# A four-layer model on one core: padding behind the vectors, later rotary angles, and latents that keep their root to the end

## The reference

```
def mla_mixer(hn, positions, w_down, q_norm, kv_norm, w_uq, w_ukv, w_o):
    c = hn @ w_down                                   # 1024 -> 384 + 256 + 32
    cq, ckv, kr = jnp.split(c, [MLA_Q_RANK, MLA_Q_RANK + MLA_KV_RANK], axis=-1)
    q  = rmsnorm_2(cq, q_norm)   @ w_uq               # 16 heads of 64 + 32
    kv = rmsnorm_2(ckv, kv_norm) @ w_ukv              # 16 heads of 64 (keys) + 64 (values)
    q_nope, q_rope = jnp.split(q, [MLA_NOPE], axis=-1)
    k_nope, v      = jnp.split(kv, [MLA_NOPE], axis=-1)
    q = concat(q_nope, apply_rope(q_rope, positions))
    k = concat(k_nope, apply_rope(kr, positions) for every head)
    o = causal_softmax_attention(q, k, v, 1 / sqrt(96))
    return o @ w_o
def rmsnorm_2(x, g):
    return x * rsqrt(mean(x * x) + 1e-6) * g
```

## Time and profile before

| | |
|---|---|
| median of 3 runs | 1326.67 us (1326.57 to 1328.77) |
| profiled execution | 1328.3 us, its span 1326.5 us |
| PE busy | 1301.6 us, 98% |
| DVE busy | 914.5 us, 69% |
| ACT busy | 756.9 us, 57% |
| DMA engines, mean | 220.61 MB in all, 166 GB/s |
| granted TensorE clock, mean | 0.994 |

### The profile page before, as it was taken

The page is one execution under the profiler, slowest core; times in us unless marked ns, Lnnn a source line. Parts: engine busy times, 40 slices in busy tenths (PEclk is TensorE's granted clock), DMA queues, the critical chain, the costliest instruction groups (busy, mean ns, idle before and its releaser), DMA issues.

```text
span 1326.5 us, 29295 instructions
## 1 busy us (share of the span) xinstructions
PE 1301.6 (98%) x12212; PEld 1269.2 (96%) x12212; DVE 914.5 (69%) x1296; ACT 756.9 (57%) x981; POOL 44.1 (3%) x37
## 2 busy tenths in 40 slices
PE   9999999999999999999999999999999999999997
PEld 8999999998999999999989899999999889999997
DVE  4779776488479876468746377666488879666556
ACT  6657665367657665357554266554376776554444
POOL 1010000010010000010000010000001001000000
PEclk9999999999999999999999999999999999999999
DMA  8455554545345555535401136553634335555520
GB/s 332 176 206 191 190 190 190 190 191 193 126 159 191 190 190 190 190 122 191 160 34 45 57 135 223 190 187 133 230 131 183 124 127 207 191 190 190 190 96 32
DMA packets 31980, 220.61 MB, mean 166 GB/s; under 512 B 3712, under 2 KB 3840, under 8 KB 6160
## 3 DMA queue, kind: packets, MB, share of 16 engines
q1 hardware_dynamic: 30672, 213.36, 44.3%
q0 software_dynamic: 784, 4.85, 1.1%
q10 hardware_dynamic: 432, 1.05, 0.2%
HBM read 218.20 MB, written 1.05 MB: 165 GB/s over the span
## 4 chain that ended last, share of the span: by engine, by line
PE 85%; DVE 9%; ACT 4%; issue 1%; DMA 1%; POOL 0%; SPq 0%; DVEq 0%; ACTq 0%; POOLq 0%
PE ps L1845 21%; PE ps L1846 21%; PE ps L1847 21%; PE ps L1856 17%; DVE w_lo L1104 3%; PE ps L1851 2%; PE ps L1852 1%; PE ps L1853 1%; ACT w_hi L504 1%; DVE xt L1156 1%; PE ps L2067 1%; DMA raw<-stream 1%; DVE xA L1166 1%; DVE xB L1166 0%; DVE xB L1128 0%
## 5 line engine op out<-in xcount | busy, mean ns | idle before, releaser
L1104 DVE TENSOR_TENSOR w_lo<-raw,w_hi 128x2048 fp32r<-128x2048 f32 x197 | 449.5, 2287 | 147.1 <-ACT w_hi L504 146.7
L504 ACT ACTIVATE w_hi<-raw 128x2048 fp32r<-128x2048 f32 x197 | 375.9, 1913 | 171.1 <-PE ps L1847 165.1
L1845 PE MATMUL ps<-xB,w_hi 128*128 128x256 f32 x1120 | 314.3, 281 | 1.7 <-DVE up_acc L1230 1.7
L1846 PE MATMUL ps<-xB,w_hi 128*128 128x256 f32 x1120 | 312.8, 279 | 0.0
L1847 PE MATMUL ps<-xB,w_lo 128*128 128x256 f32 x1120 | 312.7, 279 | 0.0
L1845 PEld LDWEIGHTS ps<-xB,w_hi 128*128 128x128 f32 x1120 | 210.5, 188 | 3.2 <-DVE up_acc L1230 1.9
L1845 PE MATMUL ps<-xA,w_hi 128*128 128x256 f32 x744 | 211.0, 284 | 1.6 <-ACT ml_v L1020 1.1
L1846 PEld LDWEIGHTS ps<-xB,w_hi 128*128 128x128 f32 x1120 | 210.5, 188 | 0.1
L1847 PEld LDWEIGHTS ps<-xB,w_lo 128*128 128x128 f32 x1120 | 210.5, 188 | 0.0
L1846 PE MATMUL ps<-xA,w_hi 128*128 128x256 f32 x744 | 207.7, 279 | 0.0
L1847 PE MATMUL ps<-xA,w_lo 128*128 128x256 f32 x744 | 207.6, 279 | 0.0
(11 more groups left out here) (287 smaller groups left out, 1869.3 us busy)
## 6 DMA issues: line engine op xcount, KB each, us to landing
raw<-stream SPq DMA_DIRECT2D x199, 1024.0 KB, 4.8
raw<-stream SPq DMA_DIRECT2D x4, 512.0 KB, 7.8
at_bias<-rel POOLq DMA_DIRECT2D x1, 2048.0 KB, 8.3
hT<-x_t SPq DMA_DIRECT2D x4, 256.0 KB, 7.0
lora_w<-lora POOLq DMA_DIRECT2D x1, 1024.0 KB, 5.1
out_t<-xt SPq DMA_DIRECT2D x4, 256.0 KB, 2.4
hcon<-hyc POOLq DMA_DIRECT2D x1, 576.0 KB, 4.1
wsT<-wst ACTq DMA_DIRECT2D x1, 512.0 KB, 4.3
```

Source lines behind the costliest of these rows:

```text
L504: nc.scalar.activation(w_hi[c.slot][:], raw[c.slot][:], ACT.Copy).then_inc(hi_made, 1)
L1104: nc.vector.tensor_tensor(w_lo[c.slot][:], raw[c.slot][:], w_hi[c.slot][:].bitcast(F32), ALU.subtract).then_inc(lo_made, 1)
L1845: nc.tensor.matmul(out, wh, xh, start=start, stop=False, skip_group_check=True)
L1846: nc.tensor.matmul(out, wh, xl, start=False, stop=False, skip_group_check=True)
```

## The change

`vec` gets 62 unused columns. It then is 3072 bytes, and all tiles behind it begin on a multiple of 1024 bytes from the first tile. `rope_angles` and the sine move behind the loop that splits the first eight chunks. The tile `ml_c` becomes `ml_tok` of the same size, of which six columns are used. The query latents are multiplied by their gain alone, straight from PSUM (ACT the high part, DVE the rest, `rest_query`), and queries are made from them without the root. `token_sums` gets the query root, and the finished key root, with one number a token on the partitions, by products with one column. The value products use the unscaled key latents, and `v_copy` multiplies by the key root. `query_root` refines the query root and leaves it negated in `ml_tok`; it goes into the maximum (one more operation of `biased_max`) and as scale into the exponent. `K_BANK` and `V_BANK` change, since banks 0 and 2 now hold the latents for longer, and PE's waits with them.

```
@@ -87 +87 @@
 GATE_BANK = (4, 6, 7, 5)
-K_BANK, V_BANK, O_BANK = (0, 1, 2, 3, 7, 0, 1, 2), (3, 7, 0, 1), (0, 1, 6, 7)
+K_BANK, V_BANK, O_BANK = (3, 7, 0, 1, 2, 3, 7, 0), (1, 2, 3, 7), (0, 1, 6, 7)
 UNITS = ((0, 1), (1, 2), (2, 4), (4, 6), (6, 8))
@@ -138 +138 @@
         hT = sb("hT", [P, KD, T])
-        vec = sb("vec", [P, NV])
+        vec = sb("vec", [P, NV + 62])
         eye_ones = sb("eye_ones", [P, 2 * P])
@@ -184 +184 @@
-                ml_c = sb("ml_c", [P, 5, T], where=f)
+                ml_tok = sb("ml_tok", [P, 5 * T], where=f)
...
@@ -608 +607 @@
                 d0 = C0[f"dn{f}"]
+                with act.Fori(0, 2) as it:
+                    for s in range(RING):
+                        split_hi(Chunk(d0 + s, it).ahead())
                 if f == 2:
...
                     nc.scalar.activation(ml_cs[:], ml_ang, ACT.Sin).then_inc(cs_made, 1)
-                with act.Fori(0, 2) as it:
-                    for s in range(RING):
-                        split_hi(Chunk(d0 + s, it).ahead())
                 if f >= 2:
@@ -627 +626 @@
                         n = 4 * m + 2 * i + t
-                        last = nc.scalar.activation(pr[:, i, lo:hi], pr[:, i, lo:hi], ACT.Exp, scale=-1.0,
-                                                    bias=st[:, 0, n:n + 1], accum_out=st[:, 1, n:n + 1])
+                        last = nc.scalar.activation(pr[:, i, lo:hi], pr[:, i, lo:hi], ACT.Exp,
+                                                    scale=ml_tok[:, t:t + 1] if a else -1.0, bias=st[:, 0, n:n + 1], accum_out=st[:, 1, n:n + 1])
                 last.then_inc(exp_made, 1)
@@ -1000 +999 @@
                 two = ps[:, s, 0:n * T].rearrange("p (b t) -> p b t", b=n)
-                nc.scalar.activation(ml_c[:, b:b + n, :], two, ACT.Copy)
                 nc.scalar.activation(xt[:, b:b + n, :], two, ACT.Square).then_inc(c_evac, 1)
+                for k, h in ((((2, 0),), (), ((0, 0), (1, 1)))[s]):
+                    nc.scalar.activation(xA[:, k, 0, :], half(s, h), ACT.Copy, scale=col("q_norm", k)).then_inc(lq_hi, 1)
                 if s < 2:
...
-            def latent_root(j, nth):
-                act.wait_ge(c_ss, nth)
-                inverse_root(ml_rs[j], half(4 + j, 0), (384, 256)[j], c_rs)
-            def round_latent(k, nth):
-                act.wait_ge(c_made, nth)
-                nc.scalar.activation(xA[:, k if k < 3 else k + 2, 0, :], xt[:, k, :], ACT.Copy).then_inc(c_hi, 1)
+            def latent_roots():
+                act.wait_ge(c_ss, 2)
+                own.mark(nc.scalar.activation(ml_tok[:, 0:2], ps[:, 4, 0:2], ACT.Ln, bias=col("eps"), scale=1.0 / 384))
+                own.mark(nc.scalar.activation(ml_tok[:, 2:4], ps[:, 4, 2:4], ACT.Copy))
+                own.wait()
+                nc.scalar.activation(ml_tok[:, 0:2], ml_tok[:, 0:2], ACT.Exp, scale=-0.5).then_inc(c_rs, 1)
...
                 t, n = divmod(i, 2)
-                nc.scalar.activation(ml_v[:, t, 512 * n:512 * n + 512], ps[:, V_BANK[i], :], ACT.Copy).then_inc(ml_evac, 1)
+                nc.scalar.activation(ml_v[:, t, 512 * n:512 * n + 512], ps[:, V_BANK[i], :], ACT.Copy,
+                                     scale=ml_tok[:, 2 + t:3 + t]).then_inc(ml_evac, 1)
@@ -1030 +1031 @@
             split_nope_hi(Chunk(c0 + 1).ahead())
-            latent_root(1, 1)
+            act.wait_ge(c_ss, 1)
+            inverse_root(ml_rs[1], half(5, 0), 256, c_rs)
             split_hi(Chunk(c0 + 2).ahead())
             latent(2)
-            round_latent(3, 1)
-            round_latent(4, 2)
-            latent_root(0, 2)
             split_hi(Chunk(c0 + 3).ahead())
+            latent_roots()
             act.wait_ge(fold_done, 1)
...
             v_copy(1)
-            for k in range(3):
-                round_latent(k, 3 + k)
             split_hi(Chunk(c0 + 4).ahead())
@@ -1260 +1258 @@
                 d0 = C0[f"dn{f}"]
-                if f == 2:
-                    rope_angles()
                 with dve.Fori(0, 2) as it:
...
                         split_lo(Chunk(d0 + s, it).ahead())
+                if f == 2:
+                    rope_angles()
                 if f >= 2:
@@ -1288 +1286 @@
-            def biased_max(a, m, bias, sign):
+            def biased_max(a, m, bias, sign, by=None):
@@ -1299 +1297 @@
                                                               ALU.add, ALU.min, st[:, 0, n:n + 1])
+                if by is not None:
+                    link(last)
+                    mx = st[:, 0, 4 * m:4 * m + 4].rearrange("p (i t) -> p i t", t=2)
+                    last = nc.vector.scalar_tensor_tensor(out=mx, in0=mx, scalar=-1.0,
+                                                          in1=by.unsqueeze(1).broadcast_to([P, 2, 2]), op0=ALU.mult,
+                                                          op1=ALU.mult)
                 last.then_inc(max_made, 1)
@@ -1732 +1736 @@
-            def scale_latent(j, nth):
-                dve.wait_ge(c_rs, nth)
-                refine(ml_rs[j], half(4 + j, 0), (384, 256)[j], ml_pr[1][:, 0, 0:T])
-                for k in ((0, 1, 2), (3, 4))[j]:
-                    gain = col("q_norm", k) if j == 0 else col("c_norm", k - 3)
-                    nc.vector.scalar_tensor_tensor(out=xt[:, k, :], in0=ml_c[:, k, :], scalar=gain, in1=ml_rs[j],
-                                                   op0=ALU.mult, op1=ALU.mult).then_inc(c_made, 1)
-            def rest_latent(k, nth):
-                dve.wait_ge(c_hi, nth)
-                x = xA[:, k if k < 3 else k + 2]
-                nc.vector.tensor_tensor(x[:, 1, :], xt[:, k, :], x[:, 0, :].bitcast(F32), ALU.subtract).then_inc(c_lo, 1)
+            def rest_query(nth, k, s, h):
+                dve.wait_ge(lq_hi, nth)
+                nc.vector.scalar_tensor_tensor(out=xA[:, k, 1, :], in0=half(s, h), scalar=col("q_norm", k),
+                                               in1=xA[:, k, 0, :].bitcast(F32), op0=ALU.mult,
+                                               op1=ALU.subtract).then_inc(lq_lo, 1)
+            def query_root():
+                dve.wait_ge(c_rs, 2)
+                y, tmp = ml_tok[:, 0:2], ml_tok[:, 4:6]
+                link(nc.vector.tensor_tensor(tmp, y, y, ALU.mult))
+                link(nc.vector.scalar_tensor_tensor(out=tmp, in0=ps[:, 4, 0:2], scalar=EPS * 384, in1=tmp, op0=ALU.add,
+                                                    op1=ALU.mult))
+                link(nc.vector.tensor_scalar(tmp, tmp, 0.5 / 384, -1.5, ALU.mult, ALU.add))
+                link(nc.vector.tensor_tensor(y, y, tmp, ALU.mult))
@@ -1760 +1767 @@
             def ml_max(m):
-                biased_max(1, m, lambda i, t: ml_bias[:, P:T] if t == 0 else ml_bias[:, 0:T], 1.0)
+                biased_max(1, m, lambda i, t: ml_bias[:, P:T] if t == 0 else ml_bias[:, 0:T], 1.0, ml_tok[:, 0:2])
@@ -1772 +1779 @@
             nc.vector.tensor_tensor(ml_kr[64:128, :], half(1, 1)[64:128], ml_cs[64:128, :], ALU.mult).then_inc(kr_made, 1)
+            rest_query(1, 2, 0, 0)
             split_nope_lo(Chunk(c0 + 1).ahead())
             scale_early(N_ML, 2, c0 + 2, 2)
-            scale_latent(1, 1)
-            k_scale(0)
-            k_scale(1)
-            rest_latent(3, 1)
-            rest_latent(4, 2)
-            k_scale(2)
-            k_scale(3)
+            dve.wait_ge(c_rs, 1)
+            refine(ml_rs[1], half(5, 0), 256, ml_pr[1][:, 0, 0:T])
+            rest_query(3, 0, 2, 0)
+            rest_query(3, 1, 2, 1)
+            for m in range(4):
+                k_scale(m)
             split_lo(Chunk(c0 + 2).ahead())
...
                 k_scale(m)
-            scale_latent(0, 2)
             split_lo(Chunk(c0 + 3).ahead())
-            for k in range(3):
-                rest_latent(k, 3 + k)
+            query_root()
             split_lo(Chunk(c0 + 4).ahead())
@@ -2383 +2388 @@
-            def latent_sums(j, evacs):
-                ks = ((0, 1, 2), (3, 4))[j]
-                pe.wait_ge(c_evac, evacs)
-                for k in ks:
-                    last = plain(half(4 + j, 0), ones, xt[:, k, :], k == ks[0], k == ks[-1])
+            def latent_sums():
+                pe.wait_ge(c_evac, 2)
+                plain(half(5, 0), ones, xt[:, 3, :], True, False)
+                plain(half(5, 0), ones, xt[:, 4, :], False, True).then_inc(c_ss, 1)
+            def token_sums():
+                pe.wait_ge(k_evac, 1)
+                for t in range(2):
+                    plain(ps[:, 4, 2 + t:3 + t], ml_rs[1][:, P * t:P * t + P], eye[:, 0:1], t == 0, True)
+                for t in range(2):
+                    for k in range(3):
+                        last = plain(ps[:, 4, t:t + 1], xt[:, k, P * t:P * t + P], ones[:, 0:1], False, k == 2)
                 last.then_inc(c_ss, 1)
...
             early_pair(N_ML, Chunk(c0), Chunk(c0 + 1), 5)
-            wide_chunk(Chunk(c0 + 2), 2, early_tile(N_ML), None, {5: lambda: latent_sums(1, 2)})
```

(21 more changed lines are left out.)

3 lines of the change are left out of this document (removed).

## The result

The changed kernel takes 1349.35 us (median of 4 runs, 1348.05 to 1350.38) against 1327.16 of the kernel before (4 runs, 1326.57 to 1328.77): a ratio of 1.0165, 95% interval 1.0152 to 1.0178. It is slower by 22 us, where 4.5 us faster was forecast. The time lies outside the range that the prediction gave. The profiled execution took 1349.58 us with a span of 1347.8.

The account below looks back on a forecast made before the run. PE, busy 98%, was taken as the bound, through matmul start-to-start time and holes. Terms -2.10 (angles), -1.56 (latents), -0.80 (padding) sum to -4.46 us: 1326.67 becomes 1322.2, range 1318.0 to 1326.0.

Parts of the forecast that it names:

- Part 1, the padding: Aligning tiles behind the vectors: nothing for products with stationary weights, -0.8 us from 480 256-column products with moving weights.
- the 512 form: Products with 512 moving weight columns, aligned: 233.04 ns, 116.52 per 256, read as no gain or loss from moving-operand alignment.
- Rival B: Big products: both operands starting on one multiple of 1024 slows 7704 matmuls to 118.36 ns; +12.9 us, 1335.9; chance 0.06.
- Part 2: Third block's down projection: moving the angles behind the weight splits removes PE's whole hole near 920 us, -2.10 us.
- Part 3: Latent stage, from first key product to first query product: making latents without the root saves 1.56 us.
- the fold: Fold product after the key products no longer waits for the third latent's square: 0.43 us stays, 0.98 goes.
- the sums: Token sums in the latent stage: 16 one-column instructions take 1.79 us instead of 1.30, so +0.49.
- the -1.37: First query product no longer waits for `v_copy(2)`, its bank being free some 5 us earlier: -1.37 us.
- the new wait of 0.3: Fifth key product waits for both `rest_query(3)` on DVE: +0.3 us.
- C: Latent stage gives nothing back, through dear one-column sums or a late split for the value product: 1324.6 us; chance 0.14.
- E: Attention: each of eight maxima comes 1.8 us later, PE stands 1.0 us eight times: 1330 us; chance 0.03.
- A: Big products: the aligned moving operand gains too, 7704 matmuls each 1.67 ns shorter; -12.9 us, 1309.3; chance 0.08.

Follow-up runs that it names:

- e1: The kernel before with only the 62 unused columns behind the vectors added: 1351.88 us, ratio 1.0184.
- m1: No full kernel: 45 groups of 24 or 48 matmuls, other engines idle, operand starts varied; 256 columns took 120.0 ns at distance 0, 113.4 at 64.
- e6: The kernel before with the later angles alone, no unused columns and the old latents: 1325.83 us, ratio 0.998.
- e7: The kernel before with the rootless latents alone, no unused columns and the old place of the angles: 1326.48 us, ratio 0.9984.
- e5: The changed kernel with 94 unused columns instead of 62, so x starts 128 bytes past a multiple of 1024: 1341.38 us, ratio 1.01 to the kernel before.
- e9: The changed kernel with 110 unused columns instead of 62, so x starts 192 bytes past a multiple of 1024: 1307.29 us, ratio 0.9861 to the kernel before.

## Why the prediction was wrong

- **What bounds the kernel** was right: PE's start-to-start time and its holes. It also named what would prove it wrong, wide steps off by more than 0.2 ns. They are off by 3.3.
- **Part 1, the padding, is the step that failed**: "So I give the wide form nothing." It was carried over from the 512 form (116.52 per 256 columns against 116.69). The two forms do not answer to the place alike: from the old place to the aligned one the 256-column step goes up by 3.3 ns and the 512-column step down by 5.2. The near equality of 116.52 and 116.69 was chance: of the places measured in both forms, it holds at the old one alone. In place of 0 the wide and natural steps of 256 columns cost +29.3 us. The -0.8 had the wrong sign: the natural form was 118.36 and became 120.00.
- **Rival B had the condition and the sign**: slower when both operands begin on one multiple. e1 and m1 show both. The reason that it gives, streams that meet at one phase, no run separates. Its size was too small, 1.67 ns on 7704 matmuls (+12.9), taken as if the natural form had already been the aligned case; it was only another place (-32 in place of +32). Measured are 3.1 ns on 9,400, and I gave it 0.06. Its "against", the 512 form, does not bear on 256 columns.
- **Part 2** was right: -2.10 forecast, the hole gone whole, e6 at -2.5 with an interval of -4.0 to -1.5. In the trace after, PE does not wait behind the moved angles. Where the hole also costs clock, as in the trace of e7, part 2 should be worth more: an estimate from its 15 steps of 213 ns is 15 x 0.096 = 1.4 us.
- **Part 3** was right in sum: -1.56 forecast, e7 at -1.8 (-3.3 to -0.8). By term, in the trace after: the fold goes from 1034.14 to 1035.20, 0.82 us over two steps where 0.43 was left to it, so -0.59 in place of -0.98; the sums take 2.02 - 0.24 = 1.78 us (1.79 forecast); behind the value products the next step comes after 0.22 us, so the -1.37 are whole; the new wait of 0.3 isn't there. Together -1.5: two errors of 0.4 and 0.3 us cancel, which is luck. C and E did not come.
- **The range** took its upper end from small waits, and left out rivals A and B, and with them the one unknown that multiplies by all matmuls. (Its inner lower bound, 1318.8, is 0.3 too low by its own terms: 1326.67 - 0.8 - 2.8 - 2.1 - 1.9 = 1319.1. Nothing rests on it.) No row of before had both operands on a multiple of 1024 with 256 columns. That was a cost with no price in the trace, and 9,400 steps stood behind each nanosecond.

## What to carry to other kernels

Where a kernel is one long stream of short equal matmuls, the distance between the stationary and the moving operand is worth a sweep. Here it moved the time of the changed kernel between 1307 and 1349 us, by 3%. Vary it over 256 bytes in steps of 32 by unused columns, and do not expect a round number to be good: 0 was among the worst. Price an edit that moves tiles by the count of all instructions that read them, and give an untested combination of form and place a range of its own instead of the value of its neighbour. Look at where the cadence settles over the whole trace, not at one stretch or at one test loop: m1 once gave 113.4 at place 64, and the kernel ran at 117.8.

## What was not expected of the hardware

- 256 columns of fp32r took between 113.3 and 121.3 ns a step at a granted clock of 1.00, by place and by what ran before, with all other engines idle.
- The cadence holds once it is there. In the seven kernels of the table other than the changed one, the undisturbed wide runs of 60 steps and more (21 or 22 a kernel, the longest 959 steps) each kept theirs to the end; it changed only across a matmul of another form or a hole. Place 64 had 113.4 and 117.7 in two runs of one loop.
- A cadence is a mean over a cycle. In the stretch of rows 3 the single steps before repeat 120, 113 or 114, 115 or 116, and 117 or 118 ns, four steps in 466 to 467. At place 128 (e5) five steps repeat, 115, 118, 121 or 122, 120 and 119 ns; at place 0 every step is 120. The cycles of four and five do not follow the three products, so they do not hang on which of the tiles is read.
- 512 columns prefer the opposite: 226.7 to 227.2 at distances 0, 256 and 512, 229.4 at 192, 232.8 at 128, 233.1 at 32, 233.4 at 64 ns.
- What stays open is the mechanism. That reads of the next stationary operand fall into the moving operand's stream at a phase that the distance sets would fit, but no run here separates the two reads. Nor is it known what would force the short cadence at place 192; if all blocks had it, e9's mean step would be about 113.5 and its profiled time some 7 us lower (an estimate, 9,400 x 0.8).
